# A two-model chain on one core: spacing of recurrence quarters and attention steps, and place of the attention store

## The reference, cut to what matters

```
def rwkv_step(S, inp):                      # scan over 512 tokens, 2 directions, 8 heads of 64
    r_t, w_t, k_t, v_t, kk_t, a_t = inp
    sa = jnp.einsum('dbhij,dbhj->dbhi', S, -kk_t)
    S = (S * w_t[..., None, :] + sa[..., :, None] * (kk_t * a_t)[..., None, :]
         + v_t[..., :, None] * k_t[..., None, :])
    return S, jnp.einsum('dbhij,dbhj->dbhi', S, r_t)

def row_block(i):                           # neighbourhood attention, 8 heads, 8 grid rows of 64
    s = jnp.einsum('bhqd,bhrkd->bhqrk', q_blk, k_blk) + bias
    prob = jax.nn.softmax(jnp.where(col_mask, s, NEG_INF), axis=(-2, -1))
    return jnp.einsum('bhqrk,bhrkd->bhqd', prob, v_blk)

x = x + (g_a * y_a + g_b * y_b) @ w_out     # y_a of the recurrence, y_b of the attention
```

## Time and profile before

| | |
|---|---|
| median of 3 runs | 2659.78 us (2657.92 to 2664.7) |
| span of the profiled execution | 2659.5 us, which is its own time |
| PE busy | 2476.8 us, 93% |
| DVE busy | 1427.9 us, 54% |
| ACT busy | 932.3 us, 35% |
| POOL busy | 220.5 us, 8% |
| chain that ended last | PE 20%, DVE 4%, ACT 2%, DMA 1% of the span followed |

### The profile page before, as it was taken

One profiled execution on the slowest core, in us unless ns is written; L12 is line 12 of the kernel. 1 busy time (PEld: TensorE's weight loads), 2 busy tenths in 40 slices (PEclk: granted clock), 3 DMA queues, 4 the chain that ended last, 5 costly groups with the idle time before them and its releaser, 6 DMA issues. The chain is left out here.

```text
span 2659.5 us, 40722 instructions
## 1 busy us (share of the span) xinstructions
PE 2476.8 (93%) x17396; PEld 1860.6 (70%) x17396; DVE 1427.9 (54%) x1943; ACT 932.3 (35%) x1264; POOL 220.5 (8%) x190
## 2 busy tenths in 40 slices
PE   8989999999999989999999999998787788989996
PEld 6767877888886657878888878877666666733332
DVE  6776446454557764455454557556666746421112
ACT  4454233232333243243232344235453533321111
POOL 1002010000010000010000020001101100133331
PEclk9999999999999999999999999999898898989998
DMA  4223322322224422222222225343021134399994
GB/s 178 85 76 119 106 76 87 107 89 105 95 95 130 127 93 80 95 82 103 100 96 95 95 110 182 120 175 81 2 54 25 20 92 144 135 369 382 398 381 174
DMA packets 100562, 343.16 MB, mean 129 GB/s; under 512 B 41376, under 2 KB 49952, under 8 KB 66592
## 3 DMA queue, kind: packets, MB, share of 16 engines
q1 hardware_dynamic: 86560, 332.13, 34.9%
q0 software_dynamic: 13824, 8.44, 1.0%
HBM read 368.29 MB, written 30.93 MB: 150 GB/s over the span
## 5 line engine op out<-in xcount | busy, mean ns | idle before, releaser
L566 PE MATMUL bank<-xg_hi,w_hi 128*128 128x512 f32 x1504 | 597.6, 397 | 12.0 <-DVE xg_lo L588 12.0
L566 PE MATMUL bank<-xg_hi,w_lo 128*128 128x512 f32 x1504 | 586.4, 390 | 0.0
L566 PE MATMUL bank<-xg_lo,w_hi 128*128 128x512 f32 x1504 | 586.4, 390 | 0.0
L553 DVE TENSOR_TENSOR w_lo<-w_raw,w_hi 128x2048 fp32r<-128x2048 f32 x165 | 378.7, 2296 | 192.8 <-ACT w_hi L549 192.7
L549 ACT ACTIVATE w_hi<-w_raw 128x2048 fp32r<-128x2048 f32 x165 | 314.3, 1905 | 247.2 <-PE bank L566 217.6
L566 PEld LDWEIGHTS bank<-xg_hi,w_hi 128*128 128x128 f32 x1504 | 283.0, 188 | 78.5 <-DVE w_lo L553 12.0
L566 PEld LDWEIGHTS bank<-xg_lo,w_hi 128*128 128x128 f32 x1504 | 283.0, 188 | 64.1 <-issue 6.0
L566 PEld LDWEIGHTS bank<-xg_hi,w_lo 128*128 128x128 f32 x1504 | 282.9, 188 | 59.3
L566 PE MATMUL bank<-f_h_hi,w_hi 128*128 128x512 f32 x384 | 151.3, 394 | 0.0
L566 PE MATMUL bank<-f_h_hi,w_lo 128*128 128x512 f32 x384 | 150.5, 392 | 0.0
L566 PE MATMUL bank<-f_h_lo,w_hi 128*128 128x512 f32 x384 | 149.0, 388 | 0.0
(11 more groups left out here) (487 smaller groups left out, 4253.1 us busy)
## 6 DMA issues: line engine op xcount, KB each, us to landing
w_raw<-stream SPq DMA_DIRECT2D x165, 1024.0 KB, 4.8
e_over_ring<-expert_rows SPq DMA_DIRECT2D x70, 1024.0 KB, 10.3
e_w_raw<-expert_rows SPq DMA_DIRECT2D x26, 1024.0 KB, 9.9
p_spill<-p_stage SPq DMA_DIRECT2D x36, 256.0 KB, 2.2
na_bias<-bias_na SPq DMA_DIRECT2D x32, 160.0 KB, 4.4
mix_gate<-p_spill SPq DMA_DIRECT2D x16, 256.0 KB, 3.4
e_w_raw<-y_rows SPq DMA_DIRECT2D x8, 512.0 KB, 7.1
rw_rkv<-p_spill SPq DMA_DIRECT2D x12, 256.0 KB, 6.2
```

Source lines behind the costliest of these rows:

```text
L553: V.tensor_tensor(ring(m)["lo"][m % SLOTS][:, :], ring(m)["raw"][m % RAW][:, :], ring(m)["hi"][m % SLOTS][:, :].bitcast(F32), ALU.subtract ...
L566: return T.matmul(out_ap, lhsT, rhs, start=first, stop=last, skip_group_check=True)
```

## The change

It changes two numbers and moves one store.

```
-    PREP_STEPS, DIR_STEPS, TAIL_STEPS, NEXT_AT = 8, 22, 5, 15
+    PREP_STEPS, DIR_STEPS, TAIL_STEPS, NEXT_AT = 8, 22, 5, 16
@@ side_by_side
-            if step * 7 % 10 < 7:
+            if step * 8 % 10 < 8:
                 advance(heads)
@@ sp_mixers, attention
+            def store_out(t):
+                Y.wait_ge(*act_na.at("out", 2 * t + 1))
+                Y.dma_start(y_spill[1, :, t, :], na_out[:, :]).then_inc(*yb_store.mark(t))
...
+                    if t and half == 0:
+                        store_out(t - 1)
...
-                if t < 3:
-                    Y.wait_ge(*act_na.at("out", 2 * t + 1))
-                    Y.dma_start(y_spill[1, :, t, :], na_out[:, :]).then_inc(*yb_store.mark(t))
```

## The result

The changed kernel takes **2615.39 us** (median of 4 runs, 2614.13 to 2616.33), the kernel before 2660.34 us beside it; the ratio is 0.9829, 95% interval 0.9815 to 0.9843.

A forecast was written before the change was run, and what follows sets the result against it. The prediction saw no engine full, but short chains between in-order engines, bound by who stands behind whose wait. Terms A to H summed to -15.6 us on 2659.5, giving 2644 us; range 2628 to 2664.

The forecast's parts named there:

- A: Joins of attention's pairs: with the store behind the next loads, DVE's waits for `na_bias` go, -14.2 us.
- B: MN products: new quarter's R and A now stand behind DVE's copies; half of PE's waits go, -5.5 us, bounds -10.9 and 0.
- F: Quarters 1 to 3 each begin a round later: three added single-quarter rounds at 3.5 us, +10.5 us, bounds +6.2 and +19.
- G: Attention moved forward 1.17 units: 8.7 us more DVE work, 39% hidden in idleness, +5.3 us, bounds 0 and +8.7.
- H: Quarters 0 to 2: scan steps sharing a round with attention's scores, six instead of five, +2.3 us, bounds -5 and +12.
- C: Last scan: attention ends nine rounds before the scan's end instead of two after it, -10 us, bounds -11.5 and -6.
- D: Last quarter before its scan: one attention unit's scores leave the 38.5 us stretch, -3 us, bounds -8 and 0.
- E: Tail: ACT's two `w_hi` splits, which held up the copy of y, come earlier, -1 us.
- The middle gives it back: Rival, chance 0.20: only the store and the end pay, added rounds and attention cost the rest; about 2658 us.
- Slower through ACT's exponentials: Rival, chance 0.13: attention's exponentials delay the recurrence's copies on ACT; 2674 us, or 2665 with half; periods about 103 us.
- The clock: Rival, chance 0.05: emptier last scan makes the combine's first 16 us begin at PE's low clock, +16 us; 2660 us.

The follow-up runs named there:

- Putting R and A back: Changed kernel with direction 0's R, A, K and B one round earlier on DVE in quarters 1 to 3, ahead of the MN copies: 2630.3 us.
- 16 alone: Kernel before with a new quarter every 16 rounds instead of 15, attention in 7 of 10 rounds, store in its old place: 2655.6 us.
- At 17: Changed kernel with a new quarter every 17 rounds instead of 16: 2645.2 us.
- Alone 8 of 10: Kernel before with attention in 8 of 10 rounds instead of 7, a quarter every 15 rounds, store in its old place: 2647.5 us.
- The run three steps later: Changed kernel with attention three steps later in every round, its DVE steps beside the MN copies: 2631.2 us.
- the run one step ahead: Changed kernel with attention one step further on in every round: 2621.8 us.
- rests in 4 to 7: Changed kernel with attention, from the first new quarter on, resting in rounds 4 to 7 of each quarter instead of 8 of 10: 2609.6 us.
- the run with the store alone: Kernel before with only the store moved behind the loads, a quarter every 15 rounds, attention in 7 of 10: 2645.2 us.

## Why the prediction was right and wrong

The forecast missed by 28.9 us, and 27.4 of them are the middle's: its terms (A, B, F, G, H) sum to -1.6, and it lost 29.0. The steps that failed are G, with H, and B. G priced attention's extra DVE work by the average idle share of DVE and called it a cost of 5.3 us; in place of it the middle gained 10.7. B took PE's own waits as the most that the place of R and A can cost; putting that place back cost 15.

Adding the edits in the order store, 16, 8 splits the middle's 29.0 us by the table's sums: 15.9, 2.4 and 10.7. The order of adding matters, since they work on each other.

- **A, the store, -14.2: right.** -15.0 alone. With 16 and 8 already in, it is 9.5: the loads' waits are shorter there, 9.2 us for 14.2.
- **B, the copies, -5.5, bounds -10.9 and 0: mis-sized, beyond its bound.** Putting R and A back (with K and B, one round earlier) costs 15 us at 16 rounds; at 15 the same place is worth 4. The step that failed took PE's three waits of the earlier trace rows as the most that the place can cost. The row holds only what PE lost to the copies, not the new quarter's exponentials on ACT behind the same DVE queue.
- **F, three more rounds, +10.5: not shown.** The starts take 10.4 us more with 16 alone, 11.7 with the store moved and 15.0 at 8 of 10, near the forecast, but they also hold work that stood in the joins before. B and F together were +5.0; 16 rounds changed the middle by -0.2, -2.4 (store moved), -26.2 (8 of 10) and -13.0 (both). Taking B's 15.6 us in the joins out of the last leaves 2.6 us for three rounds. At 17 the three cost 31.3.
- **G, attention moved forward, +5.3: wrong in sign, together with 16.** Alone 8 of 10 costs the middle 5.9, near the forecast, but in an execution 6.0 us over its median; with the store moved it is -0.1. At 16 it gains 20.1 with the store in its old place and 10.7 with it moved (267.6 to 256.9): the joins give 15.2 (109.8 to 94.6), the levels cost 4.7. The step hid a share of attention's DVE work by DVE's idleness over the whole stretch (39%; by the earlier trace rows it is 37%, which changes the term by 0.1). What counts is in which rounds it falls: 90.3 us of DVE stood in the joins with 7 of 10, 79.1 with 8 of 10. The run three steps later, at the same density, loses 16 us.
- **H, other coincidences, +2.3**: it counted scan steps beside scores, the right kind of thing with no price for where. G and H together were +7.6; -10.7 was measured, and H's lower bound was -5.
- **C, the last scan, -10: right.** 19.7 to 10.7 us.
- **D, -3, bounds -8 and 0: too small.** 38.5 to 30.4, -8.1. It took half of the scores' DVE work; what else left the stretch went uncounted, and no run tells what of it pays.
- **E, the tail, -1: right.** From 13.0 to 11.5 us.

Measured by these terms: A -15.9, 16 rounds -1.6 in joins and starts together and -0.8 in the levels, 8 of 10 -10.7, end -18.6 (-14 was forecast, and the store and 16 alone shorten the end too, by 3.0 and 9.4, which no term had); the stage's first rounds +2.0 and what follows the stage +1.1. The sum is -44.5, the difference of the spans.

*The middle gives it back*: no, it gave most. *Slower through ACT's exponentials*: the wait it rested on fell from 88.4 to 35.5 us; periods of 103 us were its condition (its own terms of the middle, +28.8 over three periods, would make them 107), and they are 87. *The clock*: the first 16 us of the combine are at 0.96 instead of 1.00, some 1.3 us at half clock (2 x 0.04 x 16). The rule of the Trainium skill cited there (TensorE: Matmul & The Clock Gate, What's actually happening) holds in direction (the emptier scan has 0.68 for 0.74), but has no weight here.

## What to carry to other kernels

Where two streams are interleaved by a written order, cut the stage by the order's own rounds and look for the pieces in which one engine is nearly full: here the second stream's work cost its DVE length and more in such pieces, and little elsewhere. Where the spacing changes, check that a piece still holds the same work before its length is compared. An average idle share says nothing of such a piece, and the list of waits gives only the first victim of a late step. The best time here came from putting the second stream's rests there by hand, rather than by a ratio whose pattern drifts across it.

## What the runs showed of the hardware

**In the joins the low clock was a sign, not a price.** The first join of the run one step ahead had a granted clock of 1.00 throughout and took 29.8 us; in the changed kernel it was 0.90 in 30.2 us, with rests in 4 to 7 0.83 in 29.5 us. Over the stage the time at half clock fell from about 85 to 41 us (2 x (1 - 0.89) x 388.7 and 2 x (1 - 0.94) x 343.1), but the joins' lengths don't follow it: PE is busy 20.2 us at 1.00 and 24.3 at 0.90 with nearly the same products, and what it is busy less it stands idle more. For the stage as a whole no run tells the clock's part; in the run with the store alone PE is busy 10.6 us less over the stage (302.2 to 291.6) as the waits go and the granted clock rises from 0.89 to 0.92.

```profile
1890.70:1920.50 29.80, 20.18 (x576) 15.86 (x576) 25.43 (x55) 15.45 (x36) 10.15 (x7) 1.00 0.04 12
```

**DVE beside POOL.** In the changed kernel direction 0's R takes 0.63 us (above), direction 1's R and A 1.76 and 1.75, while POOL works on the decayed B and K:

```profile
1903.05 1.76 DVE L2609 TENSOR_TENSOR rw_AR<-rw_AR,rw_rkv 128x512 f32<-128x512 f32 x1
1904.73 1.75 DVE L588 SCALAR_TENSOR_TENSOR rw_AR<-rw_AR,rw_kk 128x512 f32<-128x512 f32 x1
```

```profile
1902.65 1.60 POOL L2776 TENSOR_TENSOR rw_Kh<-rw_Kh,x 128x512 f32<-128x512 f32 x1 [9.61 <-DVE rw_K L2614]
1904.21 1.72 POOL L2778 TENSOR_TENSOR rw_Bh<-rw_Bh,x 128x512 f32<-128x512 f32 x1
```

The Trainium skill (SBUF — State Buffer, Who interferes with whom) says that a DVE instruction with two inputs in SBUF contends with a GpSimd instruction that reads SBUF. The trace agrees: 1.1 us more for each of the two. It is the same before the change (1.75 and 1.74, from 1909.29 on). In the run with R and A ahead of the copies POOL is through with B and K when direction 1's R begins, and R and A take 1.02 and 0.68 us in all three quarters; the other effects of that edit hide what this is worth, and POOL's work alone placed in other rounds wasn't tried.
